# Output projection as seven block products with low halves on two engines, and a reordered last mixing pair

## The reference, cut to what matters

```python
g_ssm, g_att = jnp.split(jax.nn.sigmoid(mix_g.astype(jnp.float32)), 2, axis=-1)
mixed = (g_ssm * y_ssm + g_att * y_att).astype(x.dtype)
x = x + mixed @ w_o                      # 512x1024 @ 1024x1024

h = rms_norm(x, g_norm_mlp)
x = x + jnp.square(jax.nn.relu(h @ w_up)) @ w_down
```

## Time and profile before

| what | us |
|---|---|
| median of three runs (lowest, highest) | 1256.88 (1256.61, 1258.34) |
| the profiled execution, device time | 1256.45 |
| its span in the trace | 1254.6 |
| TensorE busy in it | 1235.0 (98%) |
| VectorE, ScalarE, GpSimd busy | 770.7, 581.9, 408.1 |
| the last mixing pair, the output projection in the trace | from 813.9 to 868.35, to 911.9 |

### The profile page before, as it was taken

How to read it: one execution, slowest core, us unless ns; L and a number is a source line. 1 busy time by engine, 2 the same in 40 slices (tenths; PEclk the granted TensorE clock), 3 DMA queues, 4 the chain that set the end, 5 groups by cost and what they waited for, 6 DMA issues and landing times.

```text
span 1254.6 us, 19021 instructions
## 1 busy us (share of the span) xinstructions
PE 1235.0 (98%) x6652; PEld 1016.9 (81%) x6652; DVE 770.7 (61%) x1360; ACT 581.9 (46%) x1012; POOL 408.1 (33%) x270
## 2 busy tenths in 40 slices
PE   9999999999999999999999999999999999999997
PEld 7888877677888888888888888888878888888885
DVE  6945887775578877887774111111158749479387
ACT  6315476666544554455443222222366355364364
POOL 3433354545333333333333444444420110201200
PEclk9999999999999999999999999999999999999999
DMA  8532410000222232223223333335352160430601
GB/s 247 158 91 56 94 37 2 2 2 2 67 68 76 75 83 67 73 77 84 67 67 100 87 99 101 100 89 175 105 200 69 39 212 17 150 118 17 217 0 67
DMA packets 170328, 108.40 MB, mean 86 GB/s; under 512 B 25284, under 2 KB 161830, under 8 KB 170278
## 3 DMA queue, kind: packets, MB, share of 16 engines
q1 hardware_dynamic: 170038, 107.65, 29.4%
q10 hardware_dynamic: 240, 0.09, 0.0%
HBM read 104.84 MB, written 2.10 MB: 85 GB/s over the span
## 4 chain that ended last, share of the span: by engine, by line
PE 87%; DVE 5%; ACT 4%; issue 2%; POOL 1%; DMA 1%; SPq 0%; DVEq 0%; ACTq 0%; POOLq 0%
PE bank L2466 21%; PE bank L2057 16%; PE bank L2475 10%; PE bank L2063 8%; PE bank L2568 8%; PE bank L2573 4%; PE bank L2307 2%; PE bank L2485 2%; PE bank L2247 2%; PE bank L2286 2%; POOL prob L864 1%; PE bank L2108 1%; PE bank L2491 1%; PE bank L2446 1%; PE bank L2147 1%
## 5 line engine op out<-in xcount | busy, mean ns | idle before, releaser
L844 POOL TENSOR_TENSOR wlo<-raw,whi 128x1024 fp32r<-128x1024 f32 x133 | 326.3, 2453 | 679.9 <-ACT whi L1090 375.0
L1090 ACT ACTIVATE whi<-raw 128x1024 fp32r<-128x1024 f32 x96 | 101.8, 1061 | 296.9 <-PE bank L2475 158.4
L2057 PE MATMUL bank<-h_hi,whi 128*128 128x512 f32 x456 | 181.5, 398 | 0.7 <-DVE h_lo L1331 0.7
L2057 PE MATMUL bank<-h_lo,whi 128*128 128x512 f32 x456 | 177.9, 390 | 0.0
L2466 PE MATMUL bank<-h_hi,whi 128*128 128x512 f32 x384 | 150.3, 391 | 1.3 <-DVE grp L1777 0.7
L2466 PE MATMUL bank<-h_lo,whi 128*128 128x512 f32 x384 | 149.4, 389 | 0.0
L2063 PE MATMUL bank<-h_hi,wlo 128*128 128x512 f32 x456 | 112.9, 390 | 0.0
L1865 DVE TENSOR_TENSOR mt<-bank,sig 128x512 f32<-128x512 f32 x16 | 11.1, 691 | 162.1 <-PE bank L2475 162.1
L864 POOL TENSOR_SCALAR prob<-prob,rsum,gate 128x512 f32<-128x512 f32 (+3 forms) x128 | 79.4, 634 | 80.3 <-DVE rsum L1598 80.3
L1757 DVE SCALAR_TENSOR_TENSOR grp<-bank,vt,grp 128x511 f32<-128x511 f32 (+2 forms) x96 | 71.8, 748 | 51.9 <-ACT grp L1114 42.5
L2057 PEld LDWEIGHTS bank<-h_hi,whi 128*128 128x128 f32 x456 | 85.8, 188 | 20.0 <-DVE h_lo L1331 2.5
(11 more groups left out here) (321 smaller groups left out, 2539.7 us busy)
## 6 DMA issues: line engine op xcount, KB each, us to landing
raw<-in_w_in SPq DMA_DIRECT2D x71, 512.0 KB, 3.8
raw<-in_w_up SPq DMA_DIRECT2D x32, 512.0 KB, 4.1
draw<-in_w_down SPq DMA_DIRECT2D x16, 1024.0 KB, 6.3
raw<-in_w_ssm_branch SPq DMA_DIRECT2D x16, 512.0 KB, 3.6
raw<-in_w_in SPq DMA_DIRECT2D x28, 256.0 KB, 3.4
raw<-in_w_attn_branch SPq DMA_DIRECT2D x8, 512.0 KB, 3.6
raw<-in_w_o SPq DMA_DIRECT2D x8, 512.0 KB, 3.7
x_sb<-in_x SPq DMA_DIRECT2D x4, 512.0 KB, 5.2
```

The costliest lines, as they stand in the source:

```text
L844: nc.gpsimd.tensor_tensor(wlo[slot][:], raw[slot][:], whi[slot][:].bitcast(F32), ALU.subtract).then_inc(wlo_ready, units)
L1090: nc.scalar.activation(whi[slot][:], raw[slot][:], ACT.Copy).then_inc(whi_ready, 1)
L2057: T.matmul(bank[slot][:], whi[slot][:, k * P:(k + 1) * P], part[:, k, :], start=(k == 0 and n == 0), stop=False)
```

## The change

The output projection becomes seven block products in the manner of `down` (a scheme that multiplies two 2x2 block matrices with seven products of blocks instead of eight). The left operand is split by tokens (first and last 256) and by even and odd blocks of 128 mixed columns, `w_o` by even and odd blocks of rows and by left and right 512 columns. The left operands need four sums of blocks (`s_sum`, `a21`), the right ones four (`T1` to `T4`), the latter made in place of the loaded quarters (`quads`). Each product has two weight halves of 128 x 1024 values, fourteen in all, and two token blocks of 128. `WO` lists the products in order, with their pair of banks; those marked False add into what the bank holds. VectorE adds each pair of banks into `x1` when it is complete for that target (`wo_add`).

Of the fourteen low halves, VectorE writes ten and GpSimd four (`ON_POOL`: 5, 7, 9 and 11). Operands of the first product's halves use the two old slots, the others a ring of three (`wo_slot`).

The last mixing pair is taken out of the loop and reordered (`LAST_MIX`): both attention units first, then the four gate units, then the state-space units. With the attention units done, `o_hi` and `o_lo` are free for the quarters of `w_o`, and with the gate units done `h_hi` and `h_lo` for the left sums. The quarters come as eight transfers of 512 KB, six of them in the queue behind units 4 to 9 of the pair. In the loop the tile of even index is stored as `a11` (halves) and `a21` (unsplit), the odd one as `odd_hi`, `odd_lo`.

The residual is loaded at the end of the mixing, `g_norm_final` and the first `w_down` later than before; the first two `w_up` units are split within the projection. The core of the diff:

```diff
-        WO_ORDER = (0, 1, 2, 3)
...
+        LAST_MIX = ((2, 0), (2, 1), (0, 0), (1, 0), (0, 1), (1, 1), (3, 0), (4, 0), (3, 1), (4, 1))
...
+        WO = (("11", 0, True), ("21", 2, True), ("T1", 4, True), ("T2", 0, False), ("T3", 0, False), ("22", 4, False),
+              ("T4", 6, True))
+        WO_ADDS = [(0, c, 0) for c in (0, 1)] + [(1, c, 0) for c in (0, 1)] + [(2, c, 1) for c in (2, 3)]
+        WO_ADDS += [(3, c, 1) for c in (0, 1)] + [(4, c, 1) for c in (2, 3)] + [(4, c, 0) for c in (2, 3)]
+        WO_ADDS += [(5, c, 1) for c in (0, 1)] + [(6, c, 0) for c in (2, 3)]
...
+        WO_LEFT = {"T1": 0, "T2": 1, "T3": 2, "22": 3}
+        LEFT_ORDER = (2, 0, 1, 3)
...
+        WO_HALF, WO_LOWS, WO_SUMMED, WO_SOURCES, WO_FIRST = 14, 10, 8, 4, 12
+        ON_POOL = (5, 7, 9, 11)
...
+            def wo_half(name, h):
+                odd, right = name[0] == "2", name[1] == "2"
+                source = a["w_o"][0][512 * h:512 * h + 512, 512 * right:512 * right + 512]
+                sp.dma_start(quads[name][:, 2 * h:2 * h + 2, :],
+                             source.rearrange("(b e p) n -> p e b n", e=2, p=P)[:, int(odd)]).then_inc(tile_loaded[WO_TILE[name]], 16)
+            WO_HALVES = [("11", 0), ("11", 1), ("12", 0), ("22", 0), ("12", 1), ("22", 1), ("21", 0), ("21", 1)]
+            for n, (i, t) in enumerate(LAST_MIX):
+                weight, row0, c0 = MIX_WEIGHTS[i]
+                load(U_MIX + 30 + n, n % 2, columns(weight, row0, 768 + t * P + c0))
+                if n == 4:
+                    sp.wait_ge(unit_done, U_MIX + 32)
+                if n >= 4:
+                    wo_half(*WO_HALVES[n - 4])
+            for which in WO_HALVES[6:]:
+                wo_half(*which)
+            sp.wait_ge(unit_done, U_MLP)
+            sp.dma_start(x1[:], a["x"][0].rearrange("(c p) n -> p c n", p=P)).then_inc(x1_loaded, 16)
...
-                            sp.wait_ge(half_done, 14 * q)
+                            sp.wait_ge(half_done, WO_HALF + 14 * q)
+                        elif i == 0:
+                            sp.wait_ge(dlo_ready, WO_LOWS)
+                            sp.wait_ge(wo_pool_lo, len(ON_POOL))
...
+            for n in ON_POOL:
+                pool.wait_ge(dhi_ready, n + 1)
+                nc.gpsimd.tensor_tensor(wo_operand(n, 1), wo_part(WO[n // 2][0], n % 2), wo_operand(n, 0).bitcast(F32),
+                                        ALU.subtract).then_inc(wo_pool_lo, 1)
...
+            def high_wo(n):
+                name, h = WO[n // 2][0], n % 2
+                if name[0] == "T":
+                    act.wait_ge(w_sums, wo_sum_count(name, h))
+                else:
+                    act.wait_ge(tile_loaded[WO_TILE[name]], 16 + 32)
+                if n < 5:
+                    act.wait_ge(unit_done, U_MIX + (40 if n else 39))
+                else:
+                    act.wait_ge(half_done, n - 2)
+                nc.scalar.activation(wo_operand(n, 0), wo_part(name, h), ACT.Copy).then_inc(dhi_ready, 1)
+            def high_left(i):
+                act.wait_ge(u_sums, left_count(i))
+                nc.scalar.activation(s_hi[i][:], s_sum[i][:], ACT.Copy).then_inc(uhi_ready, 1)
             mix(0, first=True)
-            with act.Fori(1, 4) as m:
+            with act.Fori(1, 3) as m:
                 mix(m, first=False)
+            for n, (i, t) in enumerate(LAST_MIX[:8]):
+                split_next(3 * 80 + (MIX_LANDED + 16 * (n // 2 + 1)), U_MIX + 30 + n + 1, n % 2)
+                if i < 2:
+                    nc.scalar.activation(sig[:, 2 * t + i, :], bank[4 * t + i][:], ACT.Sigmoid).then_inc(mix_sig, 1)
+            high_m(3, 0)
+            high_left(2)
+            high_wo(0)
+            high_wo(1)
+            high_wo(2)
+            high_m(3, 1)
+            high_left(0)
...
+                act.wait_ge(raw_loaded[j], MLP_LANDED)
+                act.wait_ge(half_done, j + 1)
+                nc.scalar.activation(whi[j][:], raw[j][:], ACT.Copy).then_inc(whi_ready, 1)
+            for n in range(5, 14):
+                high_wo(n)
+                if n in (8, 12):
+                    for c in ((0, 1) if n == 8 else (2, 3)):
+                        act.wait_ge(down_added, 4 if n == 8 else 10)
+                        square2(0, early(c), 0, c, c)
+                if n in (9, 11):
+                    split_first((n - 9) // 2)
+            root_table(0)
+            second_half(0, WO_TOKENS, lambda c: (early(c), late(c)), down_added, 12, x1, xn2_first, (0, 2, 3, 4))
             for k in range(KT):
...
+            def gate_product(m, t, i, at_sig, done):
+                dve.wait_ge(mix_sig, m * 4 + (2 * t + 2))
+                dve.wait_ge(unit_done, done)
...
+            def mixed_sum(m, t):
+                dve.wait_ge(mix_part, m * 4 + (2 * t + 2))
+                if t:
+                    V.tensor_tensor(mt[:, 0, :], mt[:, 0, :], mt[:, 1, :], ALU.add).then_inc(mix_sum, 1)
+                else:
+                    V.tensor_tensor(mt[:, 0, 0:256], mt[:, 0, 0:256], mt[:, 1, 0:256], ALU.add).then_inc(mix_sum, 1)
+                    V.tensor_tensor(a21[:, bass.ds(m, 1), :], mt[:, 0:1, 256:S], mt[:, 1:2, 256:S], ALU.add).then_inc(a21_ready, 1)
...
+            def wo_sum(name, h):
+                if name == "T3":
+                    for source in ("12", "22"):
+                        dve.wait_ge(tile_loaded[WO_TILE[source]], 16 + 32)
+                    x, y2, op = wo_part("22", h), wo_part("12", h), ALU.subtract
+                elif name == "T2":
+                    dve.wait_ge(dlo_ready, h + 1)
+                    dve.wait_ge(w_sums, wo_sum_count("T3", h))
+                    x, y2, op = wo_part("T3", h), wo_part("11", h), ALU.add
+                else:
+                    dve.wait_ge(w_sums, wo_sum_count("T2", h))
+                    if name == "T4":
+                        dve.wait_ge(dlo_ready, h + 3)
+                    x, y2, op = wo_part("22" if name == "T1" else "21", h), wo_part("T2", h), ALU.subtract
+                V.tensor_tensor(wo_part(name, h), x, y2, op).then_inc(w_sums, 1)
+            def low_wo(n):
+                dve.wait_ge(dhi_ready, n + 1)
+                V.tensor_tensor(wo_operand(n, 1), wo_part(WO[n // 2][0], n % 2), wo_operand(n, 0).bitcast(F32),
+                                ALU.subtract).then_inc(dlo_ready, 1)
...
+                dve.wait_ge(uhi_ready, left_count(i))
...
+            def wo_add(n):
+                p, c, right = WO_ADDS[n]
+                dve.wait_ge(half_done, 2 * p + 2 if p < 6 or c == 3 else 13)
+                same = [k for k in range(n) if WO_ADDS[k][1:] == (c, right)]
+                if same:
+                    dve.wait_ge(down_added, same[-1] + 1)
+                V.tensor_tensor(x1[:, c, 512 * right:512 * right + 512], bank[WO[p][1] + c % 2][:],
+                                x1[:, c, 512 * right:512 * right + 512], ALU.add).then_inc(down_added, 1)
+            dve.wait_ge(mlo_ready, 3 * 2 + 2)
+            gate_product(3, 0, 1, 1, U_MIX + 31)
+            wo_sum("T3", 0)
+            wo_sum("T3", 1)
+            dve.wait_ge(unit_done, U_MIX + 36)
+            dve.wait_ge(a21_ready, 3)
+            kb = slice(0, 3)
+            a11 = [part[:, kb, :].bitcast(F32) for part in (a11_hi, a11_lo)]
+            a12 = [part[:, kb, 0:256].bitcast(F32) for part in (odd_hi, odd_lo)]
+            a22 = [part[:, kb, 256:S].bitcast(F32) for part in (odd_hi, odd_lo)]
+            two_steps(s_sum[0][:, kb, :], (a21[:, kb, :], a22[0], ALU.add), (a22[1], ALU.add))
+            two_steps(s_sum[2][:, kb, :], (a11[0], a21[:, kb, :], ALU.subtract), (a11[1], ALU.add))
+            step.wait()
+            two_steps(s_sum[1][:, kb, :], (s_sum[0][:, kb, :], a11[0], ALU.subtract), (a11[1], ALU.subtract))
+            step.wait()
+            two_steps(s_sum[3][:, kb, :], (a12[0], s_sum[1][:, kb, :], ALU.subtract), (a12[1], ALU.add))
+            gate_product(3, 0, 0, 0, U_MIX + 38)
+            mixed_sum(3, 0)
+            dve.wait_ge(a21_ready, 4)
+            dve.wait_ge(mix_sum, 7)
+            step.wait()
+            V.tensor_tensor(s_sum[2][:, 3, :], mt[:, 0, 0:256], a21[:, 3, :], ALU.subtract).then_inc(u_sums, 1)
+            mixed_low(3, 0)
+            gate_product(3, 1, 1, 3, U_MIX + 32)
+            low_left(2)
+            low_wo(0)
+            wo_sum("T2", 0)
+            wo_sum("T1", 0)
+            dve.wait_ge(mlo_ready, 3 * 2 + 3)
+            dve.wait_ge(u_sums, 1)
+            gate_product(3, 1, 0, 2, U_MIX + 40)
+            low_wo(1)
+            mixed_sum(3, 1)
+            dve.wait_ge(mix_sum, 8)
+            V.tensor_tensor(s_sum[0][:, 3, :], mt[:, 0, 256:S], a21[:, 3, :], ALU.add).then_inc(u_sums, 1)
+            dve.wait_ge(u_sums, 2)
+            step(V.tensor_tensor(s_sum[1][:, 3, :], s_sum[0][:, 3, :], a11_hi[:, 3, :].bitcast(F32), ALU.subtract))
+            step.wait()
```

(73 more changed lines are left out.)

265 lines of the change are left out of this document (138 added, 127 removed).

## The result

The changed kernel takes 1269.68 us (median of 5 runs, 1268.69 to 1270.95), the kernel before 1256.62 beside it: a ratio of 1.0104, interval 1.009 to 1.0117, so 13 us slower. The forecast was 1265.8 with a range to 1269.0: the direction and the waits that it named held, but a term that it did not have, TensorE's clock, makes up most of the difference. The profiled execution took 1270.21 us with a span of 1268.4, 13.8 more than the one before.

The account below looks back on a forecast made before the run. The prediction took TensorE, busy for 98% of the span, as the bound. Its terms, 13.6 + 2.2 - 5.44 - 1.1 = +9.3 us on 1256.45, gave 1265.8 us, range 1256.5 to 1269.

Parts of the forecast that it names:

- The wait for the quarter: Last mixing pair: VectorE waits at the T3 sums for w_o's last right quarter until E-12.7 us (E: mixing's end).
- The lock with GpSimd: VectorE's queue before the fifth product: SBUF instructions and four GpSimd low halves exclude each other, 6.7 us (bounds 0 to 9.6).
- without an exclusion: Rival on VectorE's queue: GpSimd's new instructions do not block VectorE; +0.4 us, 1256.9, no change; chance 0.12.
- let in only at a gap: Rival: GpSimd cannot enter between successive VectorE SBUF instructions, so two blocks of 2.1 us fall away; 1261.6 us; chance 0.25.
- The fifth product: Output projection: VectorE's 41.4 us queue plus 6.7 of blocking delays this product's start to E+35.4, 13.6 us late.
- The rival that VectorE is in time: At the fifth product only a 1.5 us turn is lost, so the kernel gets faster: 1251.4 us; chance 0.08.
- more lateness: Rival: a transfer landing at 6.5 us adds 1.3, hops in the eight sums 0.8; 1268 us; chance 0.05.
- The wait ahead of the seventh: Seventh product: a GpSimd up-weight low half stands before VectorE's last low half, 2.2 us more (bounds 0 to 2.4).
- Spared matmuls and end of the stage: Projection: 24 fewer matmuls, -5.44 us; its end: fewer transposes left and earlier up-weight splits, -1.1 us (between 0.75 and 1.8).

Follow-up runs that it names:

- e2: Changed kernel with VectorE's two T3 sums of w_o issued later, behind the eight sums of the mixing units: 1264.7 us, ratio 1.0063.
- e5: Changed kernel with the four quarters of w_o's right columns loaded ahead of the two of block 11: 1264.0 us, ratio 1.0067.
- e3: Changed kernel with GpSimd's four low halves replaced by writes of zeros, so the output lacks them: 1262.2 us, ratio 1.0046.
- e1: Changed kernel with TensorE's waits ahead of the fifth and seventh products filled with 24 and 9 idle matmuls: 1267.4 us, ratio 1.0081.
- e9: e7 with both up low halves moved from GpSimd to VectorE, and splits, root table and additions reordered for the turn: 1254.49 us, ratio 0.9982.
- e7: Changed kernel with right quarters loaded first, all low halves on VectorE, VectorE's and ScalarE's lists in TensorE's order: 1259.8 us, ratio 1.0024.

## Why the prediction was right and where it was wrong

- **The wait for the quarter.** Forecast: VectorE starts the T3 sums at E-12.7. Measured: 855.72, E-12.6. e2 and e5 show that the wait is passed on to the fifth product: taken out or shortened, it brings that product 4.5 and 5.4 us forward.
- **The lock with GpSimd.** Forecast 6.7 us: 2.1 in the eight sums, then 1.2, 2.1 and 1.3. Measured: 3.04 - 0.96 = 2.1, 2.42 - 1.22 = 1.2, 3.42 - 1.22 = 2.2, 2.46 - 1.22 = 1.2: 6.7 in all. e3 takes three of these four away and gets 4.4 back, about their 4.6. Both rivals on the lock fall: without an exclusion, e3 would have changed nothing, and "let in only at a gap" fails at 858.98 and 890.87, where GpSimd held VectorE between two SBUF instructions that followed each other.
- **The fifth product.** Forecast E+35.4, measured E+35.4, and not by luck: from the T3 sums to the end of addition 7 (855.72 to 903.67) VectorE worked for 47.95 us, and the forecast was 41.4 + 6.7 = 48.1. TensorE wanted it at E+21.8, so it is 13.6 late. The rival that VectorE is in time falls, and the one of more lateness too (its 1268 is near the result, its reason is absent).
- **The wait ahead of the seventh.** Forecast 2.2, measured 2.15 from the sixth's end, by the mechanism forecast: the last two low halves take VectorE 4.93 us (914.72) beside GpSimd's two up weights (912.83). The size is in part luck. The prediction had the last low half ready 0.4 us ahead of time (E+45.9 for E+46.3) and added the whole 2.2 all the same; by its own figures the term is 1.8. The trace had hardly any of that slack.
- **Spared matmuls and end of the stage.** Forecast -5.44 and -1.1. From the projection's last pair of matmuls (926.41; before 911.25) to the end of the first up unit (938.91; before 925.03) pass 12.5 us, before 13.8: -1.3.
- **The term that was missing: this step failed.** The sum counted every wait at its length and every matmul at 0.227 us. That price was read from a stage at clock 1.00, in which TensorE never stood, and then used behind waits of several us that the forecast itself had set there. The clock took 2.9 and 1.7 us; e1 gives back 3.8 of these 4.6 by filling the waits and nothing else. With the term, known only from the result, the forecast would have been 1265.8 + 4.6 = 1270.4. The range failed at the same place: its "more lateness" added hops and transfers, but no rival gave a wait a second price. In the trace of before the longest wait of TensorE is 1.3 us and no matmul runs behind a longer one, so no row there has this price. But that the clock falls when TensorE stands could be read there, at the end of the kernel, where TensorE's last matmul ends at 1245.99 (columns as in the earlier trace rows):

```profile
1246.00:1250.00 4.00, 0.00 (x0) 0.00 (x0) 2.25 (x5) 2.68 (x7) 0.00 (x0) 0.79 0.75 295
1250.00:1254.60 4.60, 0.00 (x0) 0.00 (x0) 0.92 (x2) 1.17 (x4) 0.00 (x0) 0.50 0.50 201
```

A clock of 0.50 doubles the price of a matmul, so the term could have been bounded: 5.4 us at most for the 24 matmuls behind each wait.

## What to carry to other kernels

A wait of several us on TensorE costs its length and then something more: behind the waits ahead of the fifth and the seventh product at which the clock fell, the 24 matmuls took 1.4 to 2.9 us longer. Where fewer matmuls are bought with more work on VectorE, draw up VectorE's list as a queue with its first wait, put it in the order in which TensorE asks, and keep GpSimd's reads of SBUF out of that stretch; here only all of this together brought a part of the saving (e9, 2.7 of 6.5 us). A piece that is moved off such a stretch lands beside another lock: look there too (e5, e7).
